# Position one of the second expert stage gathered alone: its rows ahead of the ranking, the next three positions in step two, and two routers' products on GpSimd

## The chip, the cores and the metric

One core of one Trainium2 chip runs the whole program in one launch. The metric is the device time of an execution in microseconds (us), the median of some runs. Engines: PE is TensorE's matmul, PEld its weight load, DVE is VectorE, ACT is ScalarE, POOL is GpSimd, SP is SyncE, which here only issues DMAs.

## The reference, cut to what matters

256 tokens (S), width 1024 (D). A first block (linear attention, dilated attention, then a mixture of 32 experts) is followed by a second block of two layers. The first layer has a dense feed-forward part, the second one a mixture of 8 experts:

```python
def moe_swiglu(x, router_w, router_b, w1, w3, w2):      # x: normed rows, 256 x 1024
    logits = (x @ router_w + router_b).astype(jnp.float32)
    top_v, top_i = lax.top_k(logits, TOP_K)              # TOP_K = 2
    top_p = jax.nn.softmax(top_v, axis=-1)
    gate = jnp.sum(jax.nn.one_hot(top_i, N_EXPERTS_2, dtype=jnp.float32) * top_p[..., None], axis=-2)
    out = jnp.zeros_like(x)
    for e in range(N_EXPERTS_2):                         # 8 experts, D_FF = 2816
        out = out + gate[..., e:e + 1] * swiglu(x, w1[e], w3[e], w2[e])
    return out

def swiglu(x, w1, w3, w2):
    return (jax.nn.silu(x @ w1) * (x @ w3)) @ w2
```

Ahead of each mixture stands a root-mean-square norm with a gain for every column, whose result goes to the router and to the experts. Everything is float32; the weights are 277 MB for these 8 experts alone.

## The kernel before

Each engine has its own list of instructions, written out by hand stage by stage; semaphores join them. The stages, in order: the first block, its router (about 316 to 330 us of the profiled execution), the stage of 32 experts ("pairs", to about 790), layer one of the second block, layer two, the second router (1363 to 1386), the stage of 8 experts ("wide", to about 2053), the end of layer two and the last norm.

**The two routers.** The residual sum is finished in quarters of 128 rows by 512 columns on DVE (`out_copy` for the first, `residual_copy`, L1864, for the second). The unnormed rows are turned on PE (L930), and copied out with the gain by DVE (`evac_half`, L948) and ACT (L946) into hT. PE multiplies that with the router's weights (L1882). In parallel `moe_gained_dve` (L3264) multiplies the rows with the gain row that `moe_gain_act` had sent for (four DVE instructions of 128x512, two for a half of the columns); ACT copies the product as the rounded upper part (L2060, semaphore moe_xh), and `lower_rows_dve` (L2065) subtracts that from the product for the lower part (moe_xl). PE later multiplies with both parts. Then DVE makes the logits (L2032), picks the best two (L1984 and what follows), and says `routed`; PE counts the hits (L1895, L1896) and does spare transposes around it, which have no use but to keep it at work (L914). In the second router DVE then works out each token's place within its expert (L1929 to L1934), ranks the experts by their number of tokens (to L1943), and puts the places in the ranked order. `rank_key_dve` prepares constants for that ranking. Expert 0 always takes position one; the ranking orders the other seven.

**The wide stage.** Eight positions of one expert each, with 3, 2, 2, 3, 3, 3, 3 and 2 lots of 32 rows; each position has two steps, one for each half of the 2816 hidden columns, so 16 steps. `select` makes one-hot matrices (L3138) for four positions at once, 96 columns each, so 128x384 for each of two token tiles. `gather` multiplies the rows with them: 8 column groups x 2 tiles x upper and lower part are 32 matmuls of 384 columns (L2904, L2905) into PSUM banks 5, 6 and 7 in turn, copied out by ACT (even groups) and DVE (odd groups) into wide_rows. `gather(0)` stands before step one, `gather(1)` before position four.

A step on PE is eight `up`s (L2973): each takes one 1.44 MB piece of weights with a gate half (k=0) and an up half (k=1), times the lots. Then come the eleven `down`s (L3003) of the step before. ACT applies silu to the gate half (`silu`, L3100), DVE multiplies (L3201), and the next step's first `up` waits for silu (moe_silu) and, for k=1, for the product. `silu` waits for `used` of the step's last `up`, both halves. ACT's table for silu is loaded just ahead of it.

**The queue of weights.** SP sends the pieces in one fixed order (`stream_ranked`, L616 to L629), each as two DMAs of 704 KB. There are 11 slots: piece n waits on SP until PE has `used` piece n-11. A step's ups are eight pieces and a position's step has four pieces for its downs. Every piece of a position other than the first needs that expert's number in the ranking (`expert_order`).

Of the kernel before, what the change touches and what calls it, by code (L numbers as in the profile page):

```python
# [127 lines left out]
def emit(nc, d, out):  # L128
    ctx = ExitStack()
    with ctx:  # L130
# [116 lines left out]
        count_steps("ple_tensor", {"moe1_half_done": 1, "ple_turned": 2, "moe2_half_done": 1})  # L247
# [1249 lines left out]
        def first_act(act):  # L1497
# [112 lines left out]
        def first_dve(dve):  # L1610
# [214 lines left out]
            evacuate(dve, "out_1", "dve", lambda j, src: out_copy(dve, j, src), hook=out_hook, behind=out_behind)  # L1825
            dve.wait_ge(evac_dve, jobs_of["out_1"][-1].evac)
            moe_gained_dve(dve, moe1, 1)
# [96 lines left out]
        def ranked_place_dve(dve):  # L1924
# [9 lines left out]
            dve.tensor_tensor(place[:, 1], place[:, 1], r_hit[:, 1, 0:NE2], ALU.mult)  # L1934
            vstep(dve, dve.tensor_tensor(o_pairs, o_key[:].unsqueeze(1).to_broadcast([P, NE2, NE2]),
# [126 lines left out]
        def lower_rows_dve(dve, f, half):  # L2062
            for t in range(NT):
                dve.wait_ge(sig("moe_xh"), 4 * (f.number - 1) + 2 * half + t + 1)
                dve.tensor_tensor(dealt(m_xl, t, half), dealt(nt_xn, t, half), f32(dealt(m_xh, t, half)), ALU.subtract).then_inc(sig("moe_xl"), 1)  # L2065
# [13 lines left out]
        def router1_dve(dve):  # L2079
            router_norm_dve(dve, "n2")  # L2080
            lower_rows_dve(dve, moe1, 1)
# [802 lines left out]
        def rows_ready(eng, f, r, c):  # L2884
            eng.wait_ge(sig(("moe_rows_upper", "moe_rows")[c % 2]), f.rows_before + KC // 2 * r + c // 2 + 1)
# [7 lines left out]
        def wide_pe(pe, f):  # L2893
            base = f.base["bucket"]

            banks = ((5, 6, 7), (4, 7, 1))
            all_rows = lambda r: [rows_ready(pe, f, r, c) for c in (KC - 2, KC - 1)]

            def gather(r):
                k = f.base["group"] + r  # L2900

                def chunk(c, t):
                    dst = ps[:, banks[r][c % 3], 0:TOGETHER * SPAN]
                    pe.matmul(dst, chunk_of(m_xh, t, c), wide_sel[:, t, :], start=(t == 0), stop=False)  # L2904
                    mm = pe.matmul(dst, chunk_of(m_xl, t, c), wide_sel[:, t, :], start=False, stop=(t == NT - 1))  # L2905
                    if t == NT - 1:
                        mm.then_inc(sig("moe_gathered"), 1)
# [3 lines left out]
                if r:  # L2911
                    pe.wait_ge(*side(0, 2))
                for t in range(NT):
                    pe.wait_ge(sig("moe_sel"), NT * k + t + 1)
                    for c in range(2):
                        chunk(c, t)
                for c in range(2, KC):
                    if c >= 3:
                        rows_ready(pe, f, r, c - 3)
                    for t in range(NT):  # L2920
                        chunk(c, t)
# [38 lines left out]
            def up(st, c, held):  # L2960
                p, r, q = st.up[c], st.bucket // TOGETHER, st.bucket % TOGETHER
                pe.wait_ge(piece_ready[p.slot], p.ready)
                if st.first and q == 0:
                    rows_ready(pe, f, r, c)
                for k in range(2):
                    if held and c == 0:
                        pe.wait_ge(sig("moe_hid" if k else "moe_silu"), held.no)
                    if c == 0 and st.first and (st.bucket, k) in ((0, 1), (TOGETHER - 1, 0)):
                        all_rows(st.bucket // (TOGETHER - 1))
# [41 lines left out]
            for s, st in enumerate(f.plan):  # L3011
# [20 lines left out]
                if k == 1 and b == TOGETHER - 2:  # L3032
                    gather(1)
# [15 lines left out]
        def wide_act(act, f):  # L3049
            base = f.base["bucket"]  # L3050

            def rows(r):
                for c in range(0, KC, 2):
                    act.wait_ge(sig("moe_gathered"), KC * (f.base["group"] + r) + c + 1)
                    act.copy(wide_rows[r][:, c, :], ps[:, (5, 6, 7)[c % 3] if r == 0 else (4, 7, 1)[c % 3], 0:TOGETHER * SPAN]).then_inc(sig("moe_rows_upper"), 1)
# [38 lines left out]
            def silu(st):  # L3094
                act.wait_ge(used, st.up[-1].n + 1)
# [8 lines left out]

            router_exp_act(act, f)
            rows(0)
            for s, st in enumerate(f.plan):
                b, k = st.bucket, st.since
                if s == 1:
                    ahead = act.mark_branch_hint_location()  # L3110
                if k == 0 and b == TOGETHER - 1:
                    rows(1)
# [18 lines left out]
        def wide_dve(dve, f):  # L3131
            base = f.base["bucket"]

            def select(r):
                if r:
                    dve.wait_ge(*side(0, 1))
                for t in range(NT):
                    dve.tensor_tensor(wide_sel[:, t, :].rearrange("p (q n) -> p q n", n=SPAN),  # L3138
# [1643 lines left out]
```

## Time and profile before

| what | us |
|---|---|
| median of 3 runs | 2100.31 (2099.98 to 2101.68) |
| the profiled execution's own time | 2101.52 |
| its span, first to last instruction | 2099.7 |
| PE busy | 1940.7 (92%) |
| PEld busy | 1323.4 (63%) |
| DVE busy | 741.6 (35%) |
| ACT busy | 584.6 (28%) |
| POOL busy | 53.9 (3%) |
| mean DMA rate | 297 GB/s over the span |

The mean granted TensorE clock is 0.987. The chain of work that ended last, followed back from the end, is 64% PE, 20% DMA, 6% DVE and 6% SP's queue. In the wide stage the DMA engines are busy all the time from 1465 us on, and the rate is 414 GB/s. A busy share is read with its stage: POOL's 53.9 us are almost all outside the two routers.

### The profile page before, as it was taken

The numbers are of one execution on the slowest core, as the hardware profiler recorded it, in microseconds if no ns is written. First come the engines' busy times: TensorE is split into PE (matmuls) and PEld (weight loads), VectorE is DVE, ScalarE is ACT, GpSimd is POOL, SyncE is SP. The second block draws the span as 40 slices with busy tenths as digits, with TensorE's granted clock in tenths as the row PEclk, the third lists the DMA queues.
The fourth block names the chain that finished last, engine by engine and source line by source line (L and its number), as shares of the span: only waits on it lengthen the run. The fifth ranks groups of instructions, "written<-read, shape, count | busy, mean of one in ns | idle before, by whom it ended". The sixth has DMA issues, their size and how long they took to land.

```text
span 2099.7 us, 40090 instructions
## 1 busy us (share of the span) xinstructions
PE 1940.7 (92%) x17704; PEld 1323.4 (63%) x17704; DVE 741.6 (35%) x1347; ACT 584.6 (28%) x938; POOL 53.9 (3%) x96
## 2 busy tenths in 40 slices
PE   9999998987988889999999999999978999999877
PEld 7778884332432237877888887766844677777535
DVE  8765663100101016785544676631000000000015
ACT  6555532000100006565443654510000000000005
POOL 0000000000000000120000003000000000000000
PEclk9999999999999999999999999989999999999999
DMA  9854468999999997345555552379999999999993
GB/s 222 206 161 141 157 214 320 421 421 421 421 421 421 421 416 245 122 136 167 184 184 184 167 152 85 140 280 357 415 414 416 414 414 415 414 415 415 412 385 147
DMA packets 226280, 622.79 MB, mean 297 GB/s; under 512 B 34086, under 2 KB 118694, under 8 KB 199984
## 3 DMA queue, kind: packets, MB, share of 16 engines
q1 hardware_dynamic: 221200, 611.86, 77.0%
q10 hardware_dynamic: 4288, 6.16, 0.8%
q8 instruction: 142, 2.33, 0.5%
q0 software_dynamic: 608, 2.10, 0.3%
q14 instruction: 42, 0.34, 0.0%
HBM read 614.43 MB, written 3.54 MB: 294 GB/s over the span
## 4 chain that ended last, share of the span: by engine, by line
PE 64%; DMA 20%; DVE 6%; SPq 6%; ACT 2%; issue 2%; DVEq 0%; POOL 0%; ACTq 0%; POOLq 0%
PE ps L2973 15%; DMA ring<-in_w_gate 8%; PE ps L3003 6%; SPq L629 5%; DMA ring<-in_w_down 5%; PE ps L719 5%; PE ps L721 5%; PE ps L720 5%; PE ps L2674 4%; DMA ring<-in_moe_w 4%; PE ps L729 2%; PE ps L730 2%; PE ps L733 2%; PE ps L2689 2%; DMA arena<-in_w_gate 1%
## 5 line engine op out<-in xcount | busy, mean ns | idle before, releaser
L2973 PE MATMUL ps<-ring,arena 128*32 128x352 f32 x3648 | 285.5, 464 | 24.5 <-DMA ring<-in_moe_w 17.5
L759 DVE TENSOR_TENSOR ring_parts<-ring,high_parts 128x2048 fp32r<-128x2048 f32 (+2 forms) x117 | 262.0, 2245 | 93.9 <-ACT high_parts L755 93.0
L2973 PEld LDWEIGHTS ps<-ring,arena 128*32 128x32 f32 x3648 | 160.1, 111 | 139.9 <-issue 36.5
L755 ACT CAST high_parts<-ring 128x2048 fp32r<-128x2048 f32 (+2 forms) x117 | 217.6, 1863 | 30.9 <-PE ps L721 28.4
L3201 DVE TENSOR_TENSOR arena<-ps,arena 128x1056 f32<-128x1056 f32 (+1 forms) x16 | 17.9, 1121 | 579.5 <-ACT arena L3100 550.2
L721 PE MATMUL ps<-high_parts,arena_parts 128*128 128x512 f32 (+1 forms) x494 | 194.5, 394 | 0.0
L719 PE MATMUL ps<-high_parts,hT_parts 128*128 128x512 f32 (+1 forms) x472 | 191.8, 406 | 0.0
L720 PE MATMUL ps<-ring_parts,hT_parts 128*128 128x512 f32 (+1 forms) x472 | 185.2, 392 | 0.0
L2674 PE MATMUL ps<-ring,arena 128*64 128x512 f32 x584 | 144.8, 596 | 21.3 <-DMA ring<-in_w_gate 11.8
L3003 PE MATMUL ps<-ring,arena 128*32 128x256 f32 (+1 forms) x2460 | 144.8, 362 | 12.8 <-DMA ring<-in_moe_w 12.2
L3100 ACT ACTIVATE arena<-ps,arena 128x352 f32<-128x352 f32 x42 | 20.4, 552 | 442.2 <-PE ps L2973 442.1
L3003 PEld LDWEIGHTS ps<-ring,arena 128*32 128x32 f32 x2460 | 111.3, 110 | 34.4 <-DMA ring<-in_moe_w 11.2
L2973 PE MATMUL ps<-arena 128*32 128x352 f32 x1456 | 114.2, 460 | 6.1 <-DMA arena<-in_moe_w 6.1
L730 PE MATMUL ps<-high_parts,arena_parts 128*128 128x512 f32 (+1 forms) x290 | 112.2, 388 | 0.0
L729 PE MATMUL ps<-high_parts,hT_parts 128*128 128x512 f32 (+1 forms) x272 | 107.2, 396 | 0.8 <-ACT arena L1492 0.8
L721 PEld LDWEIGHTS ps<-high_parts,arena_parts 128*128 128x128 f32 x494 | 93.1, 188 | 22.3
L2674 PEld LDWEIGHTS ps<-ring,arena 128*64 128x64 f32 x584 | 48.0, 137 | 91.1 <-issue 91.0
L2674 PE MATMUL ps<-arena 128*64 128x512 f32 x384 | 89.0, 604 | 15.6 <-DMA arena<-in_w_up 9.4
L719 PEld LDWEIGHTS ps<-high_parts,hT_parts 128*128 128x128 f32 x472 | 89.2, 189 | 20.8 <-issue 2.2
L720 PEld LDWEIGHTS ps<-ring_parts,hT_parts 128*128 128x128 f32 x472 | 89.3, 189 | 18.5
L2973 PEld LDWEIGHTS ps<-arena 128*32 128x32 f32 x1456 | 63.2, 110 | 50.0 <-issue 12.3
L3003 PE MATMUL ps<-arena 128*32 128x256 f32 (+1 forms) x1392 | 85.3, 362 | 4.6 <-DMA hT<-in_moe_w 3.3
(679 smaller groups left out, 2531.6 us busy)
## 6 DMA issues: line engine op xcount, KB each, us to landing
ring<-in_moe_w SPq DMA_DIRECT2D x255, 704.0 KB, 17.7
arena<-in_moe_w SPq DMA_DIRECT2D x110, 704.0 KB, 17.7
ring<-in_w_gate SPq DMA_DIRECT2D x39, 1024.0 KB, 27.3
ring<-in_w_down SPq DMA_DIRECT2D x35, 1024.0 KB, 27.4
ring<-in_w_up SPq DMA_DIRECT2D x34, 1024.0 KB, 27.3
ring<-in_w_in SPq DMA_DIRECT2D x104, 256.0 KB, 4.6
arena<-in_w_up SPq DMA_DIRECT2D x26, 1024.0 KB, 26.4
arena<-in_w_down SPq DMA_DIRECT2D x24, 1024.0 KB, 26.5
```

The source lines that it names most:

```text
L629: sp.dma_start(dst, src).then_inc(piece_ready[p.slot], 16)
L719: pe.matmul(dst, a_hi, b_hi, start=first, stop=False, skip_group_check=True)
L720: pe.matmul(dst, a_hi, b_lo, start=False, stop=False, skip_group_check=True)
L721: return pe.matmul(dst, a_lo, b_hi, start=False, stop=last, skip_group_check=True)
L729: pe.matmul(dst, x_hi, w_hi, start=first and i == 0, stop=False, skip_group_check=True)
L730: pe.matmul(dst, x_lo, w_hi, start=False, stop=False, skip_group_check=True)
L733: mm = pe.matmul(dst, x_hi, w_lo, start=False, stop=last and i == len(x) - 1, skip_group_check=True)
L755: act.copy(high_flat(p), raw_flat(p)).then_inc(upper, 1)
L759: dve.tensor_tensor(low_flat(p), raw_flat(p), f32(high_flat(p)), ALU.subtract).then_inc(split, 1)
L2674: mm = pe.matmul(ps[rows, bank, :], pair_rows[:, c0 + i, q * P + a * HALF:q * P + (a + 1) * HALF], w[a][:, i, :], start=(c0 + i == 0), sto ...
L2973: mm = pe.matmul(ps[32 * s:32 * s + 32, UPS[k] + g, 0:LANE], x_rows, p.bars[k][:, s * LANE:(s + 1) * LANE], start=(c == 0), stop=(c == KC ...
L3003: mm = pe.matmul(ps[32 * s:32 * s + 32, g // 2, g % 2 * 256 + c:g % 2 * 256 + c + n], hidT[:, g, j, :], w, start=(st.first and j == 0 and ...
```

## The change

Three parts.

First, in both routers the product with the gain (four instructions) moves from DVE to POOL (`rows_pool`), with the second half of the lower part (two instructions); the first half of the lower part stays on DVE. The gain row is sent for one hook earlier. `rank_key_dve` moves ahead of the evacuation of the residual.

Second, in the second router the DVE makes the one-hot matrices of position one (two instructions of 128x96) right after the places, and PE gathers its 96 columns alone (32 matmuls of 96 columns into banks 5 and 6, copied out by one ACT and one DVE instruction). The ranking follows on DVE beside step one (`ranks_dve`). The 288 columns of the next three positions are gathered in step two, four matmuls behind each of its eight ups (banks 0 and 1), and copied out there. The downs of step one wait for the last of these copies.

Third, `silu` waits for `wide_gated`, which PE signals after the gate half (k=0) of the last up. The other edits change names and counts of semaphores (`ple1_turned`).

```diff
@@ out_hook and first_dve (router one; router two alike)
-                if i == n_ab + 13 and phase:
+                if i == n_ab + 12 and phase:
                     moe_gain_act(act, moe1)
-                    moe_gained_dve(dve, moe1, 0)
-            def out_behind(dve, j):
-                if j.q == 2:
-                    lower_rows_dve(dve, moe1, 0)
-            moe_gained_dve(dve, moe1, 1)
             evac_half(dve, "dve", "n2", g2T, None, 1, (6, 7))
@@ ranked_place_dve
             dve.tensor_tensor(place[:, 1], place[:, 1], r_hit[:, 1, 0:NE2], ALU.mult)
+            dve.drain()
+            for t in range(NT):
+                dve.tensor_tensor(wide_sel[:, t, 0:SPAN], slot_no[:, 0:SPAN], r_place[:, t, 0:1].to_broadcast([P, SPAN]), ALU.is_equal)\
+                    .then_inc(sig("moe_sel"), 1)
+        def ranks_dve(dve):
             ...
@@
+        def rows_pool(pool, f):
+            for half in range(2):
+                pool.wait_ge(sig("act_moved"), 16 * f.number)
+                pool.wait_ge(evac_dve, jobs_of["out_1" if f is moe1 else "out_1_2"][2 * half + 1].evac)
+                moe_gained(pool, half)
+            lower_rows(pool, f, 1)
@@ router1_dve, router2_dve
-            lower_rows_dve(dve, moe2, 0)
-            lower_rows_dve(dve, moe2, 1)
-            rank_key_dve(dve)
+            lower_rows(dve, moe2, 0)
@@ wide_pe
+            def gather_first():
+                pe.wait_ge(sig("moe_xh"), 4 * f.number)
+                pe.wait_ge(sig("moe_xl"), 4 * f.number)
+                for h in range(2):
+                    for t in range(NT):
+                        pe.wait_ge(*sel_ready(f, FIRST, t))
+                        for c in range(4):
+                            for rows in (m_xh, m_xl):
+                                mm = pe.matmul(ps[:, 5 + h, c * SPAN:(c + 1) * SPAN], chunk_of(rows, t, 4 * h + c), wide_sel[:, t, 0:SPAN],
+                                               start=(rows is m_xh and (t, c) == (0, 0)), stop=(rows is m_xl and t == NT - 1),
+                                               skip_group_check=True)
+                    mm.then_inc(sig("moe_gathered"), 1)
+            def chunk(part, c):
+                n = len(WIDE_BANKS[part])
+                if c >= n:
+                    rows_ready(pe, f, part, c - n)
+                for t in range(NT):
+                    ...
+                    pe.matmul(dst, chunk_of(m_xh, t, c), sel, start=(t == 0), stop=False)
+                    mm = pe.matmul(dst, chunk_of(m_xl, t, c), sel, start=False, stop=(t == NT - 1))
+                mm.then_inc(sig("moe_gathered"), 1)
@@ up, down, the loop
+                    if k == 0 and c == KC - 1:
+                        mm.then_inc(sig("wide_gated"), 1)
+                    if st.own == 1:
+                        all_rows(REST)
                 if s == 0:
-                    gather(0)
+                    gather_first()
                 for i in range(KC):
                     up(st, i, held)
+                    if s == 1:
+                        chunk(REST, i)
@@ silu
-                act.wait_ge(used, st.up[-1].n + 1)
+                act.wait_ge(*ended("wide_gated", st.own))
@@ wide_dve
-            select(0)
-            rows(0)
+            first_rows()
+            ranks_dve(dve)
+            expert_order_dve(dve)
+            select(REST)
             hot_kept()
-            expert_order_dve(dve)
             ...
                 if s == 1:
+                    rows(REST)
                     dve.memset(wide_zeros, 0.0).then_inc(sig("row_numbers"), 1)
```

`router_exp_act` now stands behind ACT's copy of the first rows, and ACT's `rows(REST)` ahead of the silu of step two.

## Rows read from the trace of the kernel before

**Rows 1.** Windows: us, PE, PEld, DVE, ACT, POOL busy, granted clock, DMA share, GB/s.
```profile
1465.00:1530.00 65.00, 65.00 (x1044) 51.81 (x1036) 3.61 (x4) 3.20 (x7) 0.00 (x0) 1.00 1.02 414
1530.00:2030.00 500.00, 460.99 (x7030) 311.39 (x7022) 30.81 (x30) 24.58 (x55) 3.87 (x4) 1.00 1.02 414
350.00:355.00 5.00, 5.00 (x26) 1.65 (x24) 0.00 (x0) 0.00 (x0) 0.00 (x0) 1.00 1.02 433
```

**Rows 2.** DMA issues of 1453 to 1463 us, then of 1471 to 1482 us.
```profile
arena<-in_moe_w SPq DMA_DIRECT2D x6, 704.0 KB, 6.9
...
ring<-in_moe_w SPq DMA_DIRECT2D x10, 704.0 KB, 13.6
```

**Rows 3.** The chain of waits: start us, us, what.
```profile
1529.62 19.06 DMA ring<-in_moe_w
```

**Rows 4.** Timeline of DVE, first router: start us, us of the group, instruction.
```profile
316.02 2.16 DVE L3264 TENSOR_TENSOR arena<-x,arena 128x512 f32<-128x512 f32 x2
318.08 0.89 DVE L948 TENSOR_SCALAR hT<-ps,g2T 128x256 f32<-128x256 f32 x2
321.94 0.17 DVE L1984 TENSOR_TENSOR arena<-arena 128x8 f32<-128x8 f32 x1
```

**Rows 5.** POOL's group by form (all of it), and DVE beside and without POOL.
```profile
L3836 POOL TENSOR_TENSOR hT<-arena,low_b 128x512 f32<-128x512 f32 x10 | 12.7, 1278 | 141.9 <-ACTq L589 124.0 <-PE ps L3681 17.8
...
906.20 1.27 POOL L3853 TENSOR_TENSOR arena<-arena 128x256 f32<-128x256 f32 x2
...
906.54 0.42 DVE L4273 TENSOR_TENSOR arena<-arena 128x4 f32<-128x4 f32 x1 [0.25 <-ACT arena L4176]
...
915.26 0.15 DVE L4273 TENSOR_TENSOR arena<-arena 128x4 f32<-128x4 f32 x1
```

**Rows 6.** Timeline of DVE, second router.
```profile
1364.69 2.16 DVE L3264 TENSOR_TENSOR arena<-x,arena 128x512 f32<-128x512 f32 x2
1368.38 2.50 DVE L2065 TENSOR_TENSOR arena_parts<-arena,arena_parts 128x512 fp32r<-128x512 f32 x4
1372.01 0.17 DVE L1984 TENSOR_TENSOR arena<-arena 128x16 f32<-128x16 f32 x1
1377.69 1.03 DVE L3138 TENSOR_TENSOR arena_parts<-slot_no,arena 128x384 fp32r<-128x384 f32 x2
```

**Rows 7.** Timeline of PE, second router to the first up.
```profile
1365.64 0.96 PE L1882 MATMUL ps<-r_w,hT 128*128 128x8 f32 x8
...
1375.31 2.16 PE L914 MATMUL ps<-ident 128*128 128x128 f32 x9
...
1378.40 0.66 PE L2904 MATMUL ps<-arena_parts 128*128 128x384 f32 x1 [0.93 <-DVE arena_parts L3138]
...
1385.60 0.34 PE L2904 MATMUL ps<-arena_parts 128*128 128x384 f32 x1
1385.78 0.34 PE L2905 MATMUL ps<-arena_parts 128*128 128x384 f32 x1
1386.04 0.80 PE L2973 MATMUL ps<-ring,arena 128*32 128x352 f32 x8
```

**Rows 8.** Windows around the two stretches of a lower clock.
```profile
1369.00:1382.50 13.50, 12.43 (x51) 11.65 (x51) 8.30 (x43) 2.14 (x4) 0.00 (x0) 0.50 0.60 245
1420.00:1423.40 3.40, 3.40 (x28) 1.58 (x24) 3.18 (x8) 0.00 (x0) 0.59 (x1) 0.51 0.69 282
```

**Rows 9.** Timeline, step one to step two: ACT's table load and PE's next ups.
```profile
1416.55 1.28 ACT L3100 ACT_TABLE_LOAD   x1 [3.39 <-PE ps L2973]
...
1419.44 5.45 PE L2973 MATMUL ps<-ring,arena 128*32 128x352 f32 x48 [2.96 <-ACT arena L3100]
```

**Rows 10.** Timeline of PE: ups, full-height matmuls between them, ups.
```profile
1399.68 4.32 PE L2973 MATMUL ps<-ring,arena 128*32 128x352 f32 x56
...
1403.93 1.52 PE L2927 MATMUL ps<-arena,arena_parts 128*96 128x2 f32 x16
1405.38 7.31 PE L2973 MATMUL ps<-arena 128*32 128x352 f32 x96
```

More of the change, by code:

```diff
@@ L2080, in router1_dve @@
             router_norm_dve(dve, "n2")
-            lower_rows_dve(dve, moe1, 1)
+            lower_rows(dve, moe1, 0)
             dve.wait_ge(sig("router_psum"), 1)
@@ L2882, in stage_pairs, with sel_ready, gathered, rows_ready @@
             return (lambda pe: pairs_pe(pe, f)), (lambda act: pairs_act(act, f)), (lambda dve: pairs_dve(dve, f)), no_pool
-        def rows_ready(eng, f, r, c):
-            eng.wait_ge(sig(("moe_rows_upper", "moe_rows")[c % 2]), f.rows_before + KC // 2 * r + c // 2 + 1)
+        FIRST, REST, SECOND = 0, 1, 2
+        WIDE_BANKS = {REST: (0, 1), SECOND: (4, 7, 1)}
+        def sel_ready(f, part, t):
+            return sig("moe_sel"), NT * (f.base["group"] + part) + t + 1
+        def gathered(f, part, c):
+            return sig("moe_gathered"), KC * f.base["group"] + (c // 4 + 1 if part == FIRST else 2 + KC * (part - 1) + c + 1)
+        def rows_ready(eng, f, part, c):
+            odd = c // 4 if part == FIRST else c % 2
+            eng.wait_ge(sig(("moe_rows_upper", "moe_rows")[odd]), f.rows_before + (1 if part == FIRST else 1 + KC // 2 * (part - 1) + c // 2 + 1))
+        def wide_columns(part):
+            return slice(SPAN, TOGETHER * SPAN) if part == REST else slice(0, TOGETHER * SPAN)
+        def wide_chunk(part, c):
+            cols = wide_columns(part)
+            return wide_rows[part // 2][:, c, cols], ps[:, WIDE_BANKS[part][c % len(WIDE_BANKS[part])], 0:cols.stop - cols.start]
+        def wide_first(h):
+            return wide_rows[0][:, 4 * h:4 * h + 4, 0:SPAN], ps[:, 5 + h, 0:4 * SPAN].rearrange("p (c n) -> p c n", c=4)
         def side(r, k, psum=False):
@@ L2894, in wide_pe, with all_rows @@
             base = f.base["bucket"]
[L2896 to L2907, printed above, removed]
+            def all_rows(part):
+                for c in (3, 7) if part == FIRST else (KC - 2, KC - 1):
+                    rows_ready(pe, f, part, c)
@@ L2963, in up @@
                 if st.first and q == 0:
-                    rows_ready(pe, f, r, c)
+                    rows_ready(pe, f, SECOND if r else FIRST, c)
                 for k in range(2):
@@ L3032, in wide_pe @@
                 if k == 1 and b == TOGETHER - 2:
-                    gather(1)
+                    pe.wait_ge(*side(0, 2))
+                    for c in range(KC):
+                        chunk(SECOND, c)
                 if k == 1 and b == f.buckets - 1:
@@ L3050, in wide_act, with first_rows, rows @@
             base = f.base["bucket"]
-            def rows(r):
+            def first_rows():
+                act.wait_ge(*gathered(f, FIRST, 0))
+                act.copy(*wide_first(0)).then_inc(sig("moe_rows_upper"), 1)
+            def rows(part):
                 for c in range(0, KC, 2):
-                    act.wait_ge(sig("moe_gathered"), KC * (f.base["group"] + r) + c + 1)
-                    act.copy(wide_rows[r][:, c, :], ps[:, (5, 6, 7)[c % 3] if r == 0 else (4, 7, 1)[c % 3], 0:TOGETHER * SPAN]).then_inc(sig("moe_rows_upper"), 1)
+                    act.wait_ge(*gathered(f, part, c))
+                    act.copy(*wide_chunk(part, c)).then_inc(sig("moe_rows_upper"), 1)
             def gate(r):
@@ L3110, in wide_act @@
                     ahead = act.mark_branch_hint_location()
+                    rows(REST)
                 if k == 0 and b == TOGETHER - 1:
-                    rows(1)
+                    rows(SECOND)
                     gate(1)
@@ L3222, in wide_dve @@
                     ahead = dve.mark_branch_hint_location()
+                    rows(REST)
                     dve.memset(wide_zeros, 0.0).then_inc(sig("row_numbers"), 1)
@@ L3225, in wide_dve @@
                 if k == 0 and b == TOGETHER - 1:
-                    rows(1)
+                    rows(SECOND)
                 if k == 0 and b == 1:
-                    select(1)
+                    select(SECOND)
                 product(st)
@@ L3263, in moe_gained_dve @@
                 rows, gain = [a.rearrange("p (i c) -> p c i", c=KC) for a in (x[:, t, cols], m_gain[:, cols])]
-                dve.tensor_tensor(dealt(nt_xn, t, half), rows, gain, ALU.mult).then_inc(sig("moe_xg"), 1)
+                pool.tensor_tensor(dealt(nt_xn, t, half), rows, gain, ALU.mult).then_inc(sig("moe_xg"), 1)
         def moe_gain_act(act, f):
@@ L4439, in hook @@
                         return
+                    if l and i == 0:
+                        moe_gain_act(act, moe2)
                     if l == 0 and i < 2:
```

71 lines of the change are left out of this document (32 added, 39 removed).

## The prediction

> **What bounds the kernel now.** I read the windows first, to find the stage's limit, then the DMA issues, then the chain and the timelines of each engine around the change. From 1465 us on the DMA engines are busy all the time at 414 GB/s, with the clock at its upper level [rows 1]: to the end of the wide stage (about 2030) the weights set the pace, though PE looks busy, and the chain passes through DMAs there, one of 19.06 us [rows 3]. Before that it is PE. The reader is to see that in the landing times: pieces issued up to 1463 land 6.9 us later, so little else is queued, and SP sends a piece only when PE has given back its slot. Of those issued from 1471 on it is 13.6 us [rows 2]: now a queue stands ahead of the DMA engines, and it never empties again. So the end of the kernel is the time at which PE has given back the slots of the first steps, plus the rest at a fixed rate. An us lost or won by PE before about 1464 counts in full; one after it counts nothing. The stage of 32 experts is alike: from 350 us DMA is full at 433 GB/s [rows 1], and a shift of router one is a shift of the whole.
>
> **Router one (L3264, L2065 to POOL).** Two products that stand ahead of `evac_half` (L948) take 2.16 us, the last until 318.1 [rows 4]. Without them L948 can begin when PE's transposes are ready, at best about 1 us earlier. On POOL one instruction of this shape took 1.278 us [rows 5]. The rows of the second half are complete at 316.0, so POOL is through with its two products at 318.6; ACT's copies follow, and the two lower parts on POOL end near 322. In that time DVE makes logits and top two, which stand at 321.94 now [rows 4]. The question is whether they run beside POOL undisturbed. The trace has an answer in another stage: a small DVE product with two inputs in SBUF takes 0.15 us by itself (915.26) and 0.42 us when it starts 0.34 us into a POOL group (906.54) [rows 5]. So they hold each other up, and I let DVE's first product wait for the end of POOL's current instruction: L1984 comes at about 323.3 in place of 321.94, less 0.4 of the earlier start. Loss 1.0; bounds -1.0 (no hold-up at all) and +2.0 (two of POOL's instructions).
>
> The Trainium skill, "SBUF — State Buffer", section "Who interferes with whom", says that a DVE instruction with two inputs in SBUF and a GpSimd instruction that reads SBUF exclude each other for the whole of one of them. That speaks against the change, and the trace agrees by the 0.42 against 0.15 us of [rows 5]. By that rule the two routers come out as in this sum, and without it as in rival one, 3.3 us lower.
>
> **Router two.** Gone from DVE ahead of the logits: two of four lower parts (half of 2.50), the products' 2.16, of which some 0.9 stood in the way of L948, and `rank_key` (about 0.5, between the end of L2065 at 1370.9 and the logits) [rows 6]. That is 2.65 at most. POOL again overlaps the logits with one lower part; a hold-up of one instruction is 1.28, so 1.4 are left. Behind it: before, the ranking and two 384-wide selects (until 1378.7, from which PE waited 0.93) were last; now the selects are small and come before the ranking, and PE's nine spare transposes (2.16 from 1375.31, to 1377.5) end last [rows 6, 7]. PE thus gains the other 0.93, no more. Together -2.3; bounds -4.4 (free of POOL, transposes cut into too) and -0.3 (two POOL instructions and more).
>
> **The first gather.** Before, 32 matmuls of 384 columns lasted from 1378.40 to 1386.04: 7.64 us [rows 7], mostly at the lower clock: it was 0.50 until 1382.5 [rows 8]. At the upper clock two neighbours are 0.18 apart (1385.60, 1385.78) [rows 7]. Of 96 columns the price is the weight load's, 128 columns: eight matmuls of 8 columns took 0.96, 0.11 to 0.12 apart, at the upper clock; nine transposes took 2.16, 0.21 apart with the last one's tail off, at the lower [rows 7]. 32 x 0.21 = 6.7. I take the lower clock, for the gather before raised it only near its end and this one streams a quarter of its columns. So -0.9; bounds -4.0 (32 x 0.115) and -0.8.
>
> **The first ups at the lower clock.** Before, step one began at the full clock. If it now begins low it loses as long as the clock takes to rise. The stretch at 1420.0 to 1423.4 stood at 0.51 for 3.4 us under the same ups [rows 8], so half the work of 3.4 us, 1.7, is lost; with the end of the gather +1.9. Bounds 0 and +2.7.
>
> **Silu's earlier start.** A step's last up is 48 matmuls, at (7.31 - 0.2) / 96 = 0.074 apart [rows 10] 3.55 us. Silu waits for all of them now, and PE then stands 2.96 us until 1419.44 for a table load of 1.28 and silu [rows 9]. With the signal after k=0 this starts 1.8 earlier: -1.8. That leaves a pause of 1.2, and the lower clock from 1420.0 on, which came behind the pause [rows 8], should not come: another -1.7. Bound of this last: 0, in that the other executions (median 1.2 below the profiled one) may not have it. Later steps gain nothing: they are behind the DMAs.
>
> **The gather in step two.** 32 matmuls of 288 columns, which have no stand-in. 384 columns are 0.18 apart, the weight load's floor is 0.115; between them, by columns, 0.135: 4.3 us. It is put behind each of eight ups, and a change between ups of 32 columns and full-height matmuls costs something: from 1399.68 to 1405.38 there are 56 ups (4.14) and 16 matmuls of L2927, which by their own 1.52 less a tail are 0.085 apart, 1.36: 0.2 is left for going and coming [rows 10]. I take 0.25 for each of eight, 2.0; bounds 0.15 and 0.5. So +6.3 (5.5 to 8.3). It comes before 1464 and nothing hides it: step two's ups run at 0.074 x 48 = 3.5 us a piece, the pace of the DMAs, and every piece slot is given back that much later.
>
> **The wait ahead of step one's downs.** PE must have the last copy of the REST rows, a DVE or ACT copy of 288 columns after the last chunk, some 0.5 plus the crossing: +0.7 (0.5 to 1.0). DVE's queue there (`rows(REST)` ahead of `product`) holds nobody else; ACT's copies stand ahead of step two's silu, which is not due until its c=7. The ranking on DVE moves beside step one: SP needs `expert_order` for position two's pieces, due after 28 us of step one; it is hidden. The gates, which now come behind the ranking on DVE, are wanted by L2927 at 1403.93, 18 us into step one [rows 10], and the ranking and a select together are under 3 us (two 384-wide selects are 1.03) [rows 6]; they would cost only what they came later than that. The gain row's DMA on ACT's queue is issued one hook earlier and takes nobody's place.
>
> **Sum.** +1.0 - 2.3 - 0.9 + 1.9 - 3.5 + 6.3 + 0.7 = +3.2. The profiled execution of 2101.5 becomes 2104.7; the median stands 1.2 below that: 2103.5. As the 1.7 of the clock may not be there to be gained, I say 2104.0. The gather is cut in two, and what leaves the start comes back in step two, at a higher price and still ahead of the point from which the DMAs set the pace.
>
> **Rivals.** (1) The other side: POOL and DVE do not hold each other up here. Router one then gives -1.0, router two -3.6, so the sum is 3.3 less: 2100.2 for the median. If moreover the earlier work keeps the clock up, so that the gather takes 3.7 and the ups start at full speed (3.1 and 1.9 less), it is 2095.2, faster. For it: most of POOL's work ends before the top two's chain, and the small instructions copy from PSUM. Against it: the 0.42 of [rows 5], and a clock of 0.50 right here [rows 8]. 0.22 in all, 0.14 and 0.08 for its two forms; it decides at L1984 in each router. (2) Dearer pieces: POOL's product with the interleaved column order takes some 2.1 us in place of 1.28, and a change of shape 0.5: 0.8 x 2 in each router and 2.0 in step two, with a last copy late for a matmul bank: +9.4, 2109.7 to 2110.5. For it: no row of [rows 5] has that order on POOL. 0.10. (3) The gather in step two is hidden after all, for DMA, not PE, is last in step two: 3.2 - 6.3 = -3.1, so 2097.2. Against it are the 6.9 us of landing at 1453 to 1463 [rows 2]. 0.08.
>
> **How the numbers follow.** 0.60 stays for the forecast, with its own range of 2101.5 to 2107. Some 0.2% (4.2 us) is what can be told from no change: faster is below 2096.1, slower above 2104.5. Faster: 0.08 and a part of (3) and the bounds, 0.12. Slower: (2) with 0.10 and 0.27 of the forecast's 0.60 that lies above 2104.5: 0.37. The rest, 0.51, is no change. The range of 2098 to 2108 leaves out rival (2) and the second form of (1), about 0.2.
>
> **What would show it.** Right: L1984 later by about 1 us in router one (measured from the last residual), earlier by about 1.4 in router two; the gather of 32 short matmuls lasting near 6.7 at a clock of 0.50; a first up within 1 us of 1383 before any shift of router one; a pause below 1.5 us between steps one and two; step two longer by 6 to 7 us on PE, and the pieces that it frees issued that much later; 414 GB/s after 1465 unchanged. Wrong: DVE instructions beside POOL at their own durations; ups at the full clock from the first; pieces of steps three and four that land no later than before although PE freed them later, which would say that the end does not hang on PE there.

## The result, and the profile after

The changed kernel takes 2108.09 us (median of 8 runs, 2106.49 to 2111.02) against 2101.74 for the kernel before in 8 runs (2099.98 to 2102.36): a ratio of 1.003, 95% interval 1.0021 to 1.0039. It is 4.4 to 8.2 us slower. Forecast were 2104.0 and a range up to 2108; the sum said +3.2. The forecast was added to the median of 3 executions of the kernel before, 2100.31; that of the 8 beside the changed kernel is 1.4 higher. Of the experiments e3, e9 and e11 below, and of the kernel before beside e9 to e12, one execution each took over 300 us more (5660.95, 3263.09, 2441.42 and 3930.01) and is left out of every median below.

The page of the changed kernel begins so:

```profile
span 2106.4 us, 40161 instructions
...
PE 1948.5 (93%) x17736; PEld 1322.5 (63%) x17736; DVE 737.9 (35%) x1338; ACT 584.7 (28%) x939; POOL 76.3 (4%) x108
```

POOL has 22.4 us more, DVE 3.7 less. A page says no more of it than that; the shares don't show the loss. What does is a ledger: one takes instructions that both kernels have, and subtracts their starts. The marks here are DVE's last residual of router one (315.30 in the kernel before), its first instruction behind router one's counts (327.94), the second residual of the last layer (1356.64, ahead of anything that router two's part changes), the first instruction behind router two's counts (1375.51), and ACT's first result of the wide stage (1497.28).

| stretch, profiled executions | changed kernel | forecast |
|---|---|---|
| up to router one | +2.03 | 0 |
| router one | +2.05 | +1.0 |
| between the routers | +1.54 | 0 |
| router two, to the counts | -0.58 | -1.4 |
| counts to the first result | +3.28 | +3.6 |
| the rest | -1.6 | 0 |
| span | +6.7 | +3.2 |

(The forecast's router two was -2.3 to the start of the gather, of which -0.9 lies behind the counts; the fifth line holds it.)

**Where no code differs.** The 2.03 ahead of router one comes at 60 to 67 us. Windows of the changed kernel, columns as in [rows 1]:

```profile
60.00:64.00 4.00, 1.27 (x11) 0.62 (x11) 3.22 (x10) 0.39 (x2) 0.00 (x0) 0.96 1.20 291
64.00:67.10 3.10, 3.10 (x34) 2.42 (x34) 0.17 (x1) 0.92 (x5) 0.00 (x0) 0.50 1.20 293
```

PE stood for nearly 3 us (1.27 busy in 4), and the granted clock is 0.50 behind it. In the profiled execution before the same wait was there and the clock stayed up:

```profile
60.00:64.00 4.00, 1.30 (x28) 1.18 (x31) 2.77 (x8) 0.37 (x1) 0.00 (x0) 1.00 1.18 291
64.00:68.00 4.00, 4.00 (x34) 3.06 (x30) 2.51 (x4) 1.49 (x6) 0.00 (x0) 1.00 1.18 291
```

Experiments with the same code there have the loss (1.2 to 2.1 us in eight of their fourteen profiled executions) or don't, and which ones does not follow the edits: all eight have a granted clock of 0.50 to 0.68 in that window, the six others 1.00, and the wait ahead of it is the same. So two single traces differ by some 2 us from this alone, and a ledger has to be read stretch by stretch. Between the routers, where no code differs either, the experiments go from -1.1 us (e13) to +5.1 (e14). Part of that goes with the clock: 1 minus the granted clock, added up over that stretch, is 6.8 us before, 6.2 in e13, 9.3 in the changed kernel and 11.8 in e14; but in e3, with +3.4, it is 8.4.

**Router one.** The timeline of DVE, then of POOL, of the changed kernel:

```profile
317.32 0.69 DVE L1853 SCALAR_TENSOR_TENSOR x<-ps,x 128x512 f32<-128x512 f32 x1 [3.89 <-PE ps L721]
319.20 0.88 DVE L948 TENSOR_SCALAR hT<-ps,g2T 128x256 f32<-128x256 f32 x2 [1.19 <-PE ps L930]
320.00 0.23 DVE L997 TENSOR_TENSOR small<-small 128x2 f32<-128x2 f32 x1
320.26 1.95 DVE L998 TENSOR_SCALAR small<-small 128x2 f32<-128x2 f32 x1
...
322.68 2.36 DVE L2074 TENSOR_TENSOR arena_parts<-arena,arena_parts 128x512 fp32r<-128x512 f32 x2
...
325.60 0.58 DVE L1985 TENSOR_TENSOR arena<-arena 128x8 f32<-128x8 f32 x1
```
```profile
318.16 4.03 POOL L3313 TENSOR_TENSOR arena<-x,arena 128x512 f32<-128x512 f32 x2 [9.82 <-DVE x L1853]
323.04 3.13 POOL L2074 TENSOR_TENSOR arena_parts<-arena,arena_parts 128x512 fp32r<-128x512 f32 x2 [0.85 <-ACT arena_parts L2061]
```

POOL's product takes 2.02 us, not 1.28. L998 is a tensor_scalar of two columns, 0.17 us before; here it lasts from 320.26 until 322.21, and POOL's second product ends at 322.19. L997 just ahead of it has two inputs in SBUF; it came at the end of POOL's first product and lost only 0.05 (0.23 for 0.18). The lower parts of DVE take 2.36 for two (1.29 before) beside POOL's, and L1985 ends with the last of these (326.18 and 326.17). L948 did come 0.9 earlier after the residual, as forecast: -0.9 + 1.8 + 1.1 + 0.4, less 0.3 of waits before it, is the 2.05.

**The wide stage.** Timeline of PE and ACT, then two pieces of the chain of waits, of the changed kernel:

```profile
1381.82 7.03 PE L2935 MATMUL ps<-arena_parts 128*128 128x96 f32 x32
1388.79 19.28 PE L3002 MATMUL ps<-ring,arena 128*32 128x352 f32 x240
...
1418.84 1.28 ACT L3141 ACT_TABLE_LOAD   x1 [1.62 <-PE ps L3002]
...
1421.72 3.76 PE L3002 MATMUL ps<-ring,arena 128*32 128x352 f32 x48 [1.19 <-ACT arena L3141]
1425.41 0.40 PE L2948 MATMUL ps<-arena_parts 128*128 128x288 f32 x1
...
1426.13 3.76 PE L3002 MATMUL ps<-arena 128*32 128x352 f32 x48
```
```profile
1457.13 0.47 DVE arena L3194
1457.85 14.52 PE ps L3036 x216
```

The gather of position one ran at 0.50 (window 1381.30 to 1391.50, below) and took 7.03. PE then stood 1.19 for silu and not 2.96. In step two a piece is 4.41 apart from the next (1421.72, 1426.13), of which the 48 matmuls are 3.54 (0.074 each): 0.87 for each insertion. The downs waited 0.75 for the last copy. The DMAs are as in [rows 1, 2], 8 us later: full at 413 GB/s from 1473, landing 5.8 us after their issue at 1461 to 1472 and 13.0 at 1479 to 1490.

```profile
1381.30:1391.50 10.20, 10.05 (x55) 7.89 (x56) 2.92 (x13) 1.97 (x3) 0.00 (x0) 0.50 0.13 50
...
1473.00:1538.00 65.00, 65.00 (x1044) 51.95 (x1040) 3.61 (x4) 3.20 (x7) 0.00 (x0) 1.00 1.02 413
```
```profile
arena<-in_moe_w SPq DMA_DIRECT2D x6, 704.0 KB, 5.8
```
```profile
ring<-in_moe_w SPq DMA_DIRECT2D x10, 704.0 KB, 13.0
```

### The profile page after: what moved, and what is told of

Read it like the earlier page. It is cut to its first block, busy times and chain, and to the rows that moved or that the text cites. A ratio compares the mean times of both kernels' runs of the same rounds, so it can differ in the third digit from the quotient of the medians.

```text
span 2106.4 us, 40161 instructions
## 1 busy us (share of the span) xinstructions
PE 1948.5 (93%) x17736; PEld 1322.5 (63%) x17736; DVE 737.9 (35%) x1338; ACT 584.7 (28%) x939; POOL 76.3 (4%) x108
## 3 DMA queue, kind: packets, MB, share of 16 engines
HBM read 614.43 MB, written 3.54 MB: 293 GB/s over the span
## 4 chain that ended last, share of the span: by engine, by line
PE 66%; DMA 20%; DVE 6%; SPq 5%; ACT 2%; issue 2%; POOL 0%; DVEq 0%; ACTq 0%; POOLq 0%
PE ps L3002 15%; DMA ring<-in_w_gate 8%; PE ps L3036 7%; DMA ring<-in_w_down 5%; PE ps L719 5%; SPq L629 5%; PE ps L721 5%; PE ps L720 5%; PE ps L2681 4%; DMA ring<-in_moe_w 3%; PE ps L729 3%; PE ps L730 2%; PE ps L733 2%; PE ps L2696 2%; DMA arena<-in_w_down 1%
```

## The experiments

The experiments ran on four chips, so each has its own executions of the kernel before beside it, whose median is given too: medians are best compared as differences from that. All ratios are to the kernel before on the same chip. They come from all those executions and aren't the quotient of the medians: for e2 the ratio gives 0.2 us and the medians 1.4. The last three columns are stretches of the ledger of one profiled execution: router one, router two to the counts, counts to the first result. That execution isn't always near the median: e2's took 2107.17 us, e5's 2096.48, e14's 2110.55.

| kernel | median us | kernel before, median us | ratio, 95% interval | r. one | r. two | wide |
|---|---|---|---|---|---|---|
| changed | 2108.09 | 2101.74 | 1.003, 1.0021 to 1.0039 | +2.05 | -0.58 | +3.28 |
| e1, router one on DVE | 2104.17 | 2101.02 | 1.002, 1.001 to 1.003 | +0.22 | -0.58 | +3.24 |
| e13, router two on DVE | 2105.67 | 2101.54 | 1.0019, 1.001 to 1.0028 | +2.05 | -1.04 | +4.72 |
| e2, both on DVE | 2102.45 | 2101.02 | 1.0001, 0.9992 to 1.001 | +0.24 | -1.02 | +4.70 |
| e9, before with POOL alone | 2105.16 | 2102.08 | 1.0011, 1.0002 to 1.002 | +2.04 | +1.06 | +0.46 |
| e10, lower parts on DVE | 2106.40 | 2102.08 | 1.002, 1.0011 to 1.003 | +1.76 | -0.92 | +3.22 |
| e14, plain order on POOL | 2104.72 | 2101.54 | 1.001, 0.9999 to 1.0021 | +0.73 | -1.47 | +4.04 |
| e3, rest gathered together | 2102.95 | 2101.02 | 1.0011, 1.0002 to 1.0019 | +2.05 | -0.18 | +0.40 |
| e4, before with silu's signal | 2098.22 | 2101.02 | 0.9983, 0.9974 to 0.9992 | 0.00 | -0.02 | -3.49 |
| e5, e2 and e3 | 2099.88 | 2100.83 | 0.9994, 0.9985 to 1.0003 | +0.20 | -0.33 | -4.99 |
| e6, e4 with wide spares in both routers | 2098.01 | 2100.83 | 0.9982, 0.9974 to 0.9991 | -0.35 | -0.43 | -4.11 |
| e7, e2 with wide spares | 2099.75 | 2100.83 | 0.9991, 0.9983 to 1.0 | -0.01 | +0.62 | -1.32 |
| e11, e5 with wide spares | 2095.05 | 2102.08 | 0.9964, 0.9951 to 0.9976 | -0.02 | +0.61 | -4.99 |
| e12, e4, early ranking constants, wide spares in router two | 2096.47 | 2102.08 | 0.9972, 0.9961 to 0.9983 | -0.02 | +0.60 | -5.32 |

**e1 and e2: the products back on DVE.** In router one (router two likewise in e2):

```diff
+                    moe_gained_dve(dve, moe1, 0)
+            def out_behind(dve, j):
+                if j.q == 2:
+                    lower_rows(dve, moe1, 0)
...
+            dve.wait_ge(evac_dve, jobs_of["out_1"][-1].evac)
+            moe_gained_dve(dve, moe1, 1)
...
-router1_act, router1_dve, lambda pool: rows_pool(pool, moe1))
+router1_act, router1_dve, None)
```

> The changed kernel with router one's products and lower parts back on DVE as before (the gain row's DMA one hook later too); router two and the wide stage as changed. Theory (POOL takes 2.02 us for a product where DVE takes 1.08, and DVE stands still beside it): the counts of router one (L1888) come 2.0 us earlier relative to the last residual, so 2108.1 becomes 2106.0; if the 0.7 to 1.3 us that the stage of 32 experts lost further on came from the same place, 2104.8. Rival (the loss of router one is chance of the clock, since 2.0 us were lost at 64 us into the profiled execution already): no change, 2108.1.

> The changed kernel with both routers' products and lower parts back on DVE; the wide stage as changed. Theory: in router two POOL freed DVE for the last residual (0.86 us) and held it up afterwards (L998 1.93 us in place of 0.17, L2074 2.37 in place of 1.25); I expect the balance to be about 0.5 to 1.0 in favour of POOL there, so this kernel is 0.5 to 1.0 above the one with router one alone put back: about 2106.0. Rival: POOL loses in router two as well, as in router one, and this kernel is 1 to 2 us below the other.

Measured 2104.17 and 2102.45. With e1 router one's 2.05 fell to 0.22; the kernel is 3.2 above its own kernel before, where the changed one was 6.35, so it gained 3.2. With e2 it gained another 1.7, so the rival of e2 holds. Without POOL the whole of the rest of the change costs what can't be told from nothing (1.0001, 0.9992 to 1.001). That is not because its parts cost nothing: see e4.

**e9 and e13: the POOL part alone, and router two alone put back.** e9 is the kernel before with `rows_pool` in both routers and `rank_key_dve` at its old place; e13 is the edit of e2 in router two only.

> The kernel before with the routers' part of the change alone: products and the second half of the lower parts on POOL in both routers, gain row one hook earlier. Theory (that part is most of the loss; undoing it in the changed kernel gave 5.7 us): 2101.0 + 4 to 5.7 = 2105 to 2106.7. Rival (undoing it helped only by where the clock then fell in the changed wide stage): 2101 to 2103.

> The changed kernel with router two alone back on DVE (router one's products and lower part stay on POOL). Theory one (POOL costs 2.0 us in router one and 0.4 in router two, in every setting; the rest of what the experiments gave is scatter of the clock between executions): 2107.5. Theory two (router two's POOL is dear because of what follows it, in that it shifts the gather to where the clock falls, 1.7 us as between the two experiments that had router one on DVE): 2106.4 or less.

e9 costs 3.1 (by ratio 2.3), between the rival's 0 to 2 and the theory's 4 to 5.7; its ledger has 2.04 + 1.06 + 0.46 = 3.6. Its router two loses 1.06 where that of the changed kernel gains 0.58, and a row tells why. Timeline of DVE, then of POOL, of e9:

```profile
1374.14 1.22 DVE L1908 COPY o_key_base<-desc 128x8 f32<-128x8 f32 x1
```
```profile
1372.20 3.14 POOL L2066 TENSOR_TENSOR arena_parts<-arena,arena_parts 128x512 fp32r<-128x512 f32 x2 [0.84 <-ACT arena_parts L2053]
```

The first copy of `rank_key_dve`, 0.17 us before, lasts until 1375.36, and POOL's lower part ends at 1375.34: 1.05 us for an instruction of 8 columns with one input. In the changed kernel it stands elsewhere.

e13 is 4.1 above its kernel before and so gains 2.2, so the second theory of that expectation is nearer: e1 and e13 together (3.2 + 2.2) are about what e2 gave at once (4.9). But the ledger of e13 does not show the 2.2: router two gains 0.46 and the stretch behind it loses 1.44, because in this execution the clock stayed low for longer: until about 1388.9, 5.3 us into step one, where the changed kernel's rose at about 1391.5, 2.7 us into it. That POOL costs 3 us where it alone is added and 5 to 6 where it is taken from the changed kernel stays open: the intervals, some 1.9 us to each side of every ratio, overlap.

**e8 and e14: the order of the columns.**

```diff
-                rows, gain = [a.rearrange("p (i c) -> p c i", c=KC) for a in (x[:, t, cols], m_gain[:, cols])]
+                rows, gain = [a.rearrange("p (c i) -> p c i", c=KC) for a in (x[:, t, cols], m_gain[:, cols])]
```

> The changed kernel, but the products with the gain read x and the gain row in plain order and not every eighth column, which puts the columns of the experts' input in another order (the routers are untouched). Theory (the order is what makes POOL's product cost 2.02 us): 1.3 us each, as for the plain 128x512 product of the trace of before, and the counts of router one come 1.4 us earlier relative to the last residual. Rival (POOL takes this long for two float32 inputs and a 3-d output in any order, its lower part of 1.57 being held up by DVE): 1.9 to 2.0 us, no change in the counts.

> The changed kernel with the products' columns in plain order on POOL (another order of the experts' input columns), now timed. Theory one: 1.3 us less in router one and as much in router two's share, so 2106 to 2106.7. Theory two (the order's cost is not on the path in router two, or the scatter hides it): 2107 to 2108.

Neither kernel puts the experts' weights in that order, so the output isn't the reference's; the number of instructions is that of the changed kernel (40161). Timeline of POOL, then of DVE, of e8 (one execution, 2108.25):

```profile
317.64 2.50 POOL L3313 TENSOR_TENSOR arena<-x,arena 128x512 f32<-128x512 f32 x2 [11.30 <-DVE x L1853]
```
```profile
319.48 0.68 DVE L997 TENSOR_TENSOR small<-small 128x2 f32<-128x2 f32 x1
320.19 0.17 DVE L998 TENSOR_SCALAR small<-small 128x2 f32<-128x2 f32 x1
...
320.83 2.37 DVE L2074 TENSOR_TENSOR arena_parts<-arena,arena_parts 128x512 fp32r<-128x512 f32 x2
```

1.25 us for one product in place of 2.02. POOL is done at 320.14. Now it is L997 that meets POOL's second product: 0.68 us for 0.18, until 320.16. L998 behind it is back at 0.17; the lower parts beside each other are as slow as before. Router one costs 0.73 and not 2.05, the 1.3 that was expected. By its own kernel before e14 is 3.2 lower than the changed kernel, more than both theories said; its executions range over 13 us (2097.59 to 2110.55), and what the rows don't give of it stays open. DVE took 1.08 for the interleaved product [rows 4].

**e10: lower parts back on DVE**, `lower_rows(pool, f, 1)` taken out of `rows_pool`.

> The changed kernel with the lower parts all on DVE and only the products on POOL. Theory (DVE is held up twice: L998 waits for the end of POOL's second product, 1.8 us, and L2074 and L1985 for POOL's lower parts, 1.1 and 0.4): without the second, DVE does four lower parts at 0.65 (2.5) in place of two at 1.18 (2.4) and 0.4: the counts come 0.3 us earlier in each router, 2107.5. Rival (the lower parts on POOL are what costs, the products nothing): 2 us less in each router, 2104.

0.3 us in each router (1.76 for 2.05, -0.92 for -0.58), as in the theory. The median fell by 1.7 (2.0 by its own kernel before), which these rows don't explain.

**e4: silu's signal alone**, put on the kernel before:

```diff
+                    if k == 0 and c == KC - 1:
+                        mm.then_inc(sig("wide_gated"), 1)
...
-                act.wait_ge(used, st.up[-1].n + 1)
+                act.wait_ge(*ended("wide_gated", st.own))
```

> The kernel before with one edit of the change: silu waits for the gate half of the last up (wide_gated) and not for both halves. Theory: 1.8 us less from the earlier start, and 1.7 less because the clock does not fall behind the shorter pause: 2098.2. Rival one (the fall of the clock comes by chance in the profiled execution): 2099.9. Rival two (the start of step two is hidden by the DMAs): 2101.7.

-3.49 in the stretch where 3.5 was said. The median is 2098.22, as forecast, but with some luck: the kernel before was 0.7 faster here than the forecast took it, so the gain is 2.8 by medians and 3.6 by the ratio. Of the change's three parts it is the only one that gains by itself. e2 is this edit, the split gather and the earlier constants of the ranking, on the same chip, and is 4.2 above e4 by medians, 3.8 by ratios (0.9992 to 1.001 against 0.9974 to 0.9992): the split gather costs at least that much, somewhat less than the routers' part (4.9 by medians, 6.1 by ratios).

**e3: the rest gathered together.**

```diff
+                if s == 1:
+                    pe.wait_ge(*side(0, 2))
+                    for c in range(KC):
+                        chunk(REST, c)
                 for i in range(KC):
                     up(st, i, held)
-                    if s == 1:
-                        chunk(REST, i)
```

> The changed kernel with the eight parts of the gather of positions two to four together ahead of the first up of step two, in the pause for silu, and copied out by DVE alone; nothing else changed. Theory (each part between two ups costs 0.87 us: 0.54 of matmuls and 0.33 of changing shape, and the pause of 1.2 us is idle): 8 x 0.87 = 7.0 becomes 8 x 0.54 + 0.3 - 1.2 = 3.4 plus some waiting for the copies (0.6 us a part in place of 0.54), so 3.0 us less, 2105.1. Rival (what counts is not PE's time there but the order of the slots): 2108. Rival (the copies ahead of the product of step one on DVE make the second half of the first up wait): 1.5 us less, 2106.6.

Timeline of PE of e3, first and last of the 32 matmuls and the ups behind them:

```profile
1421.74 0.40 PE L2952 MATMUL ps<-arena_parts 128*128 128x288 f32 x1
...
1426.81 0.29 PE L2953 MATMUL ps<-arena_parts 128*128 128x288 f32 x1
1427.03 3.77 PE L3006 MATMUL ps<-ring,arena 128*32 128x352 f32 x48
```

The whole takes 5.3 us (1421.74 to 1427.03), in place of 7.0 in pieces plus a pause of 1.2 plus 0.75 ahead of the downs: 3.6 less. The ledger has 2.9 less (0.40 for 3.28), 0.4 having gone in slower first ups (19.72 for 19.28). By its own kernel before e3 is 4.4 lower than the changed kernel, more than the 3.0 expected.

**e5, e7, e11: these together, and the clock.** e5 is e2 with e3. e7 is e2 with other spare work in router two, 6 and 3 products of 256 columns in the place of 18 and 9 transposes; e11 is all of it:

```diff
+        def spare_streams(pe, bank, n):
+            for _ in range(n):
+                pe.matmul(ps[:, bank, 0:256], ident[:], x[:, 0, 0:256], start=True, stop=True)
```

> The changed kernel with both experiments on it that helped: the routers' products back on DVE, and the gather of positions two to four together ahead of step two, copied by DVE. Theory (the two are independent, 5.7 and 4.3 us of medians): 2108.1 - 5.7 - 4.3 = 2098.1. Rival (part of either was chance of the clock between executions): 2100 to 2101.

> The changed kernel with the routers' products on DVE, and in router two the same spare products (6 and 3). Theory (the first gather at 7.0 us and the first ups are slow because of the clock, 3.4 and 1.3 us in all): with the clock up as the gather begins it takes 3.6 us; the clock may still fall behind it, since it streams a quarter of the columns, which then costs the ups 1.7: 2102.5 - 3.4 + 0.4 = 2099.5. Rival (the weight loads set the gather's pace at either clock): 2102.5, no change.

> The changed kernel with all three: products on DVE, the gather of positions two to four together ahead of step two, and in router two the spare products of 256 columns (6 and 3). Theory (all independent and each PE microsecond ahead of 1464 counts): 2099.9 - 2.7 = 2097.2. Rival (with PE this early the DMAs set the pace already in step one and two): no gain on 2099.9.

Timeline of PE, then a window, of e7:

```profile
1377.35 3.74 PE L2954 MATMUL ps<-arena_parts 128*128 128x96 f32 x32
1381.02 17.96 PE L3021 MATMUL ps<-ring,arena 128*32 128x352 f32 x240
```
```profile
1377.30:1381.00 3.70, 3.70 (x33) 3.65 (x32) 0.07 (x1) 1.64 (x2) 0.00 (x0) 1.00 0.03 14
```

The same 32 matmuls take 3.74 us at the upper clock and 7.03 at the lower, and the ups behind them 17.96 for 19.28. So the two terms on the clock, 3.3 and 1.3 us, are shown. e7 is 2.7 below e2 (2.5 by their own kernels before, 2.1 by the ratios, whose intervals overlap), near its theory. That the spare products brought the clock up is less sure, for e5 has the transposes and the same gather. Timeline of PE of e5:

```profile
1378.16 3.75 PE L2947 MATMUL ps<-arena_parts 128*128 128x96 f32 x32
```

Its granted clock was back at 1.00 from 1378. Over all profiled executions, the gather began at the upper clock in four of four with the products (e6, e7, e11, e12) and in one of twelve with the transposes (e5). Columns alone aren't separated from length either: in e7 the products fill the wait for `routed`, while in the changed kernel PE stood 2.38 us there.

e5's median is 2099.88, above the 2098.1 of its theory and just under its rival's 2100 to 2101. Its profiled execution, with the clock up, is one of its fastest, so its -4.99 is more than the median has. e11 is 2095.05, below both kernels: 0.9964 (0.9951 to 0.9976), from five executions. That is 7.0 below its kernel before, where e5 is 0.9 below; the step of 6 is more than the 2.7 of the theory, and the ledger (router two 0.9 worse, wide the same) has none of it, since e5's profiled execution had the clock up already.

**e6, e12: the same on the kernel before.**

> The kernel before with silu's earlier start, and in both routers the spare transposes behind the logits and behind the counts replaced by spare products of 256 columns in plain float32 (8 and 6 in router one, 5 and 6 in router two), which keep PE streaming. Theory (the gathers that follow lose time to the lower clock that the waits in the router bring): the granted clock is back up by the start of the gather in router two, which then takes 5.6 in place of 7.6 us, and router one's stretch ends 2 us earlier; 2098.2 less 2 to 4: 2095. Rival (the spare products at the lower clock, 0.85 us each, end after DVE and delay the counts): 2099 to 2101.

> The kernel before with silu's earlier start, the constants of the ranking prepared earlier, and in router two alone the spare products of 256 columns (6 and 4); one gather of 384 columns as before. Theory: 2098.2 less 0.5 for the constants and 1.7 for a gather of 5.9 at the upper clock that starts no later: 2096.0, the fastest so far; that the gather is not split costs less than the split. Rival (the spares end after DVE): 2098.

e6 gives nothing over e4 (2098.01; 0.9982 and 0.9983), though its ledger is 1.4 lower in the three stretches: its spares behind router two's counts end at 1381.2, 0.8 after the one-hot matrices (1380.45), something like what its rival said of the counts; the gather at the upper clock (5.9 us) is partly paid back by that. With fewer of them, e12 is 2096.47, as its theory said, 5.6 below its kernel before. Its gather of 384 columns in one piece can't be told from e11's split (0.9961 to 0.9983 against 0.9951 to 0.9976).

## Why the prediction was wrong

It was slower as the sum said (+3.2), but by 6.35, and the stated time was 4.1 too low. 1.4 of the 4.1 is that the median of three which it was added to was low. Of the 3.15 by which the sum was short, the two routers are 1.05 and 0.8; the wide stage was 0.3 less than forecast, and 1.6 is in no row. By its own steps:

- **Router one, the step that failed.** I put POOL's product at 1.278, the nearest row [rows 5], which has no interleaved input. It measured 2.02, and 1.25 in plain order (e8). And I let only DVE instructions with two inputs in SBUF be held up; L998, with one, waited 1.8 us. The term was +1.0 with a bound of +2.0; it is 2.05, at the bound. It was also put as one hold-up, of the first of the top two's products; there are three, 1.8 at L998, 1.1 at the lower parts and 0.4 at L1985. The rival "dearer pieces" named 2.1 us for this very instruction and had a chance of 0.10. With the product at 1.25 (e8) router one costs 0.73.
- **Router two.** -1.4 to the counts was -0.58, for the same two reasons. The start of the gather was forecast 2.3 early and came 2.2 early: the nine transposes took 1.3 and not 2.2, the clock being up just then. By e13 and e2 POOL is no help here either.
- **The hold-up.** What I had wrong of it was which instructions it takes. The Trainium skill, "SBUF — State Buffer", "Who interferes with whom", also says of tensor_scalar that it can take both port pairs, and can then contend with GpSimd. L998 at 1.95 us in place of 0.17 agrees with it; I had used only the sentence on two inputs. That page's rule was the right side to take: DVE was held up in all executions with POOL's part, and rival (1) is out.
- **First gather, first ups, silu.** -0.9, +1.9 and -3.5 measured -0.7, +1.3 and -3.5 (7.64 to 6.97, from its start to the first up; first up to step one's gates; e4). The lower clock that I chose there did come. One reading behind that choice was off: in the gather before the clock rose at 1382.5, a little past the middle and not near the end [rows 7, 8].
- **The gather in step two and the downs.** +6.3 and +0.7 measured +7.0 (8 x 0.87) and +0.75. The change of shape costs 0.33 and not 0.25 us.
- **1:1 ahead of 1464.** Router two and the wide terms sum to +2.7 (forecast +2.2), and the first result of the wide stage is late by 5.04 + 3.28 = 8.32; 7.1 of it stands at the next result (1565.70 before), 8.4 at that of 1910. What PE lost ahead of the DMAs' taking over was kept, to within 1.2 us. Rival (3) is out; the forecast's range left out its 2097.2 too, so more than the 0.2 that was said lay outside.

The three stretches that the change touches, as measured, sum to 2.05 - 0.58 + 3.28 = +4.75, within the interval of 4.4 to 8.2. The other 1.6 of the median are not accounted for by rows, and their cause stays open. The span's +6.7 does not account for them: 2.03 + 1.54 of it come where the code is alike, and 1.6 is given back at the end, 1.0 of it between the results of 1910 and 1996, where the DMAs are full in both.

## What to carry to other kernels

Work moved from VectorE to GpSimd was dear twice here: in its own duration, which depends on the access pattern (time the very pattern), and in what it did to VectorE's instructions beside it, the smallest ones with a single input included. When a piece of TensorE work is to be moved off a start, put it whole into a pause of TensorE rather than in parts between matmuls of another shape, and look first whether the pause itself can be shortened: one earlier semaphore gave 3.5 us in the rows. Time the parts of a change one by one: here one gain stood against two losses. And before an effect is read from one trace, look at the granted clock in both: the same router code had the first gather at 0.50 in e2 and at 1.00 in e5.

## What the runs showed of the hardware

- POOL, product of two float32 128x512: 2.02 us when both inputs are read every eighth column, 1.25 in plain order; DVE 1.08 for the interleaved one.
- A two-column tensor_scalar on DVE waited 1.8 us, until the end of POOL's instruction, in every profiled execution that had the interleaved products there (changed kernel, e1, e3, e9, e10, e13). A copy of 8 columns with one input waited 1.05 beside POOL's lower part (e9), and a product of two columns 0.5 beside the plain one (e8). DVE's L948, which reads PSUM, kept its 0.88 beside POOL.
- 32 matmuls of 96 columns with a 128-column weight load each: 3.74 us at a granted clock of 1.00 (e7), 7.03 at 0.50 (changed kernel). The weight loads alone were busy for 3.65 and 6.90 of it, so they follow the clock too.
- The same code has or has not a low stretch of the clock from one execution to the next (0.50 to 0.68 or 1.00 at 64 to 67 us behind the same wait), 1.2 to 2.1 us each time. The 11 runs of e2 range over 9.1 us (2098.08 to 2107.17), of the 32 runs of the kernel before beside them 30 over 3.0. Why e2 scatters more isn't shown.
